# Key and small columns of a hybrid layer through one dense tile, with one latent step moved among the inverse's levels

## The reference, cut to what matters

```python
proj = rmsnorm(x, norm1_g) @ w_in
(ssd_z, ssd_xbc, ssd_dt, mla_cq, mla_ckv, mla_kr, gdn_qkv, gdn_z, gdn_b, gdn_a, gate_logits) = split(proj)
y_ssd = ssd_mixer(ssd_z, ssd_xbc, ssd_dt, ...)      # decays from dt, 16 heads
y_mla = mla_mixer(mla_cq, mla_ckv, mla_kr, ...)     # latents 512 + 256, rotary key 64
y_gdn = gdn_mixer(gdn_qkv, gdn_z, gdn_b, gdn_a, ...)# inverse of a lower triangle, per head and chunk
```

## Time and profile before

| | us |
|---|---|
| median of 3 runs | 2484.85 (2478.69 to 2486.74) |
| the profiled execution | 2484.22 |
| its span, first to last instruction | 2482.4 |
| PE busy | 2391.7 |
| mean granted clock of PE | 0.987 |

### The profile page before, as it was taken

How to read it: one execution, slowest core, us unless ns; L and a number is a source line. 1 busy time by engine, 2 the same in 40 slices (tenths; PEclk the granted TensorE clock), 3 DMA queues, 4 the chain that set the end, 5 groups by cost and what they waited for, 6 DMA issues and landing times.

```text
span 2482.4 us, 48243 instructions
## 1 busy us (share of the span) xinstructions
PE 2391.7 (96%) x21350; PEld 2217.1 (89%) x21350; DVE 1424.7 (57%) x2157; ACT 1249.5 (50%) x1848; POOL 302.0 (12%) x171
## 2 busy tenths in 40 slices
PE   7989999999999899999999999999999999998999
PEld 6979998999999799899999886887789997788999
DVE  5773776665457467756655347643335554676554
ACT  5755655554466475456543367532223444354442
POOL 4214000000241220001000004200000001331000
PEclk9999999999999999999999999999999999999999
DMA  4344444555444443545553245333225532223554
GB/s 175 136 154 170 153 160 171 197 187 187 157 169 152 154 157 139 199 154 194 190 186 128 102 138 203 124 120 131 103 101 188 203 139 103 87 76 131 187 187 170
DMA packets 56064, 382.31 MB, mean 154 GB/s; under 512 B 6064, under 2 KB 9904, under 8 KB 10288
## 3 DMA queue, kind: packets, MB, share of 16 engines
q1 hardware_dynamic: 55104, 375.90, 42.2%
q10 hardware_dynamic: 752, 3.33, 0.4%
HBM read 377.11 MB, written 1.05 MB: 152 GB/s over the span
## 4 chain that ended last, share of the span: by engine, by line
PE 82%; DVE 9%; ACT 4%; DMA 2%; issue 2%; POOL 0%; DVEq 0%; ACTq 0%; POOLq 0%
PE ps L948 21%; PE ps L949 21%; PE ps L950 21%; DVE r L2226 3%; ACT r L1567 2%; PE ps L1029 1%; PE ps L1077 1%; PE ps L1031 1%; PE ps L1030 1%; DMA ring<-in_win 1%; PE ps L907 1%; PE ps L869 1%; PE ps L986 1%; PE ps L988 1%; PE ps L987 1%
## 5 line engine op out<-in xcount | busy, mean ns | idle before, releaser
L948 PE MATMUL ps<-r,r 128*128 128x256 f32 (+1 forms) x4464 | 1326.2, 297 | 5.3 <-DVE r L2283 1.9
L949 PE MATMUL ps<-r,r 128*128 128x256 f32 (+1 forms) x4464 | 1313.1, 294 | 0.0
L950 PE MATMUL ps<-r,r 128*128 128x256 f32 (+1 forms) x4464 | 1311.7, 294 | 1.0 <-issue 1.0
L2226 DVE TENSOR_TENSOR r<-ring,r 128x1024 fp32r<-128x1024 f32 (+2 forms) x558 | 677.6, 1248 | 519.6 <-ACT r L1567 519.4
L948 PEld LDWEIGHTS ps<-r,r 128*128 128x128 f32 x4464 | 842.4, 189 | 42.1 <-issue 9.5
L950 PEld LDWEIGHTS ps<-r,r 128*128 128x128 f32 x4464 | 842.0, 189 | 25.0
L949 PEld LDWEIGHTS ps<-r,r 128*128 128x128 f32 x4464 | 842.4, 189 | 24.2 <-issue 0.5
L1567 ACT ACTIVATE r<-ring 128x1024 fp32r<-128x1024 f32 (+1 forms) x614 | 613.2, 1039 | 294.5 <-DMA ring<-in_fo 69.3
L3164 POOL TENSOR_TENSOR slab<-slab 128x512 f32<-128x512 f32 (+1 forms) x20 | 28.6, 1432 | 1231.2 <-ACT slab L1683 1210.9
L3116 POOL TENSOR_TENSOR r<-ring,r 128x1024 fp32r<-128x1024 f32 x56 | 133.2, 2400 | 226.3 <-ACT r L1567 216.4
L2315 DVE SCALAR_TENSOR_TENSOR slab<-ps,v,slab 128x255 f32<-128x255 f32 (+1 forms) x168 | 68.0, 474 | 81.6 <-ACT slab L1635 81.6
(11 more groups left out here) (344 smaller groups left out, 2530.1 us busy)
## 6 DMA issues: line engine op xcount, KB each, us to landing
ring<-in_win SPq DMA_DIRECT2D x76, 1024.0 KB, 4.8
ring<-in_ada SPq DMA_DIRECT2D x48, 1024.0 KB, 4.8
ring<-in_fi SPq DMA_DIRECT2D x44, 1024.0 KB, 4.8
ring<-in_fo SPq DMA_DIRECT2D x36, 1024.0 KB, 4.8
ring<-in_wup SPq DMA_DIRECT2D x32, 1024.0 KB, 4.7
ring<-in_wdn SPq DMA_DIRECT2D x32, 1024.0 KB, 4.8
ring<-in_hin SPq DMA_DIRECT2D x20, 1024.0 KB, 4.8
ring<-in_nqkv SPq DMA_DIRECT2D x12, 1024.0 KB, 4.8
```

The source lines that it names most:

```text
L948: self.mm(o, hi[:, k - k0, cs], xh, k == 0, False)
L949: self.mm(o, hi[:, k - k0, cs], xl, False, False)
L950: i = self.mm(o, lo[:, k - k0, cs], xh, False, k == last)
L2226: self.tt(K.low(p), K.raw(p), K.high(p).bitcast(F32), ALU.subtract).then_inc(*self.up("w_lo_v", p))
```

## The change

The 32 small columns and the 64 of the rotary key become one chunk of 128 columns (32 of them zero). It is computed as a dense tile, and ACT writes it to `few`, a free tile of `gate`. PE then turns the two token halves for `sm` (bank `smT`) and spreads the key's halves over the partitions by 8 matmuls with columns of the identity (bank `kr`), which ACT copies into `lat`'s tiles 6 and 7. `win` has 74 chunks instead of 76, and `lat` three steps instead of four. In the list of turns, the 5th piece of `small` comes one `qkv` step later and the rest of it after `qk`'s first piece, the first latent step goes from behind the recurrence to between the first and second level of the inverse, with its chunks prepared ahead of the first level, and the two others stay among the decays.

```diff
--- before.py
+++ after.py
@@ -28,7 +28,7 @@
 
 
 MATS = {
-    "win": (1024, 9728, 128, 1), "wsm": (1024, 32, 32, 1), "wuq": (512, 1536, 256, 1), "wuk": (256, 1024, 512, 1),
+    "win": (1024, 9472, 128, 1), "wsm": (1024, 128, 128, 1), "wuq": (512, 1536, 256, 1), "wuk": (256, 1024, 512, 1),
     "wuv": (256, 1024, 512, 1), "wso": (1024, 1024, 128, 1), "wmo": (1024, 1024, 128, 1), "wgo": (1024, 1024, 128, 1),
     "wo": (1024, 1024, 128, 1), "wup": (1024, 4096, 128, 1), "wdn": (4096, 1024, 128, 4),
     "ada": (1024, 6144, 128, 1), "nqkv": (1024, 3072, 128, 1), "no": (1024, 1024, 128, 1),
@@ -407,6 +407,7 @@
         self.xn = self.pair(A, 8, T)
         self.mixed, self.gate, self.y, self.sq, self.rs = (A(8, T) for _ in range(5))
         self.one = self.mixed[:, 0, 0:128]
+        self.few = self.gate[:, 1:2, :]
         self.sm, self.sp, self.sa, self.sb_, self.sc = A(2, 32), A(2, 24), A(2, 24), A(2, 24), A(2, 24)
         self.smask = A(48)
         self.beta, self.dA, self.cum = A(2, 8), A(2, 24), A(2, 24)
@@ -514,16 +515,16 @@
         win = lambda key, c0, c1, kind, **more: J.update({key: Job((key, L), "win", L, range(c0, c1), T, self.xn, n1, kind, **more)})
         out = lambda key, ys, kind, **more: J.update({key: Job((key, L), key, L, range(8), T, ys, halves((key, L)), kind, source=self.y, **more)})
         win("qkv", 0, 16, "conv", lead=2, dst=self.g_acc, taps="gw", bias=None, free=[])
-        J["wsm"] = Job(("wsm", L), "wsm", L, [0], 32, self.xn, n1, "rows", to=[self.sm[:, m, :] for m in range(2)])
-        win("z", 44, 52, "act", dst=self.g_z, func=ACT.Silu)
-        win("gz", 36, 44, "act", dst=self.z2, func=ACT.Silu, fine=True, free=lambda g: [("gd_v", ("y", L, 6))])
-        win("gate_g", 68, 76, "act", dst=self.mixed, func=ACT.Sigmoid)
+        J["wsm"] = Job(("wsm", L), "wsm", L, [0], T, self.xn, n1, "act", dst=self.few, func=ACT.Copy)
+        win("z", 42, 50, "act", dst=self.g_z, func=ACT.Silu)
+        win("gz", 34, 42, "act", dst=self.z2, func=ACT.Silu, fine=True, free=lambda g: [("gd_v", ("y", L, 6))])
+        win("gate_g", 66, 74, "act", dst=self.mixed, func=ACT.Sigmoid)
         out("wgo", self.ys_g, "mix", source_at=lambda i: ("gd_v", ("y", L, i)), gate=self.mixed, gate_of=("gate_g", L), first=True)
         win("xbc", 16, 28, "conv", dst=self.s_acc, taps="cw", bias="cb", free=[("gd_v", ("qg", L, 1, 1)), ("gd_p", ("uu", L, 3))])
-        win("lat", 28, 36, "act", dst=self.lat, func=ACT.Copy)
-        win("gate_s", 52, 60, "act", dst=self.gate, func=ACT.Sigmoid)
+        win("lat", 28, 34, "act", dst=self.lat, func=ACT.Copy)
+        win("gate_s", 50, 58, "act", dst=self.gate, func=ACT.Sigmoid)
         out("wso", self.ys_s, "mix", source_at=lambda i: ("sd_v", ("y2", L, i)), gate=self.gate, gate_of=("gate_s", L), first=False)
-        win("gate_m", 60, 68, "act", dst=self.gate, func=ACT.Sigmoid, free=lambda g: [("ev_v", ("gated", ("wso", L), g))])
+        win("gate_m", 58, 66, "act", dst=self.gate, func=ACT.Sigmoid, free=lambda g: [("ev_v", ("gated", ("wso", L), g))])
         J["wuq"] = Job(("wuq", L), "wuq", L, range(6), T, self.qn, xk(("qn", L)), "copy", dst=self.q12)
         J["wuk"] = Job(("wuk", L), "wuk", L, range(2), T, self.kn, xk(("kn", L)), "copy", dst=self.kT)
         J["wuv"] = Job(("wuv", L), "wuv", L, range(2), 512, self.kn, xk(("kn", L)), "rows", to=[self.vt[:, m, :] for m in range(2)])
@@ -572,20 +573,20 @@
         yield ("ada0", 1)
     first = lambda turn: [turn] if L == 0 else []
     yield from [("norm1", None), ("qkv", 2), ("small", 1), ("qkv", 1), ("small", 2), *first(("angles", 1)), ("qkv", 1), ("small", 1), *first(("angles", 1)),
-                ("qkv", 1), ("small", 1), *first(("angles", 1)),
-                ("qkv", 1), ("small", None), *first(("conditions", None)), ("qk", 1), ("qkv", 1), ahead("z", 1), ("qk", None), ("qkv", 1), ahead("z", 3),
+                ("qkv", 1), *first(("angles", 1)),
+                ("qkv", 1), ("small", 1), *first(("conditions", None)), ("qk", 1), ("qkv", 1), ahead("z", 1), ("small", None), ("qk", None), ("qkv", 1), ahead("z", 3),
                 ("qkv", None), ("z", 2), ahead("z", 5), ("gdn", 1), ahead("z", 7)]
     for fill in ("z", "z", "gate_g", "gate_g"):
         yield from [("gdn", 1), (fill, 1)]
     yield from [("gdn", 1), ("gate_g", 1), ("gdn", 1), ("gate_g", 1), ("gate_s", 1), ("gdn", 1), ("gate_s", 1),
-                ("gdn", 1), ("gate_s", 1), ("ada0", 2), ("gdn", 4), ahead("gate_s", 6), ("ada0", 1), ("gdn", 4), ahead("gate_s", 7),
+                ("gdn", 1), ("gate_s", 1), ("ada0", 2), ahead("lat", 1), ("gdn", 4), ("ada0", 1), ("lat", 1), ahead("gate_s", 6), ("gdn", 4), ahead("gate_s", 7),
                 ("gdn", 4), ("ada0", 1)]
     yield from [("gate_s", 1), ("gdn", 1), ("xbc", 1)]
     for n in range(5):
         yield from [("gdn", 1), ("xbc", 1)]
         if n in (0, 2):
             yield ("ada0", 1)
-    yield from [ahead("lat", 3), ("gdn", 1), ("xbc", 1), ("lat", 1), ("xbc", 1), ("lat", 1), ahead("lat", 5), ("gdn", None), ahead("lat", 7), ("ssd", 1)]
+    yield from [ahead("lat", 3), ("gdn", 1), ("xbc", 1), ("xbc", 1), ("gdn", None), ahead("lat", 5), ("ssd", 1)]
     for fill in ("lat", ("lat", "split wgo"), None, "wgo", "wgo", ("mla", "wgo"), None, "wgo"):
         yield ("ssd", 1)
         if fill:
@@ -1080,7 +1081,15 @@
 
     def small(self, L):
         K, up, at, e = self.K, self.up, self.at, self.e
-        yield from self.rows(K.jobs1[L]["wsm"])
+        yield from self.dense(K.jobs1[L]["wsm"])
+        P = self.open("smT", L)
+        self.wait_ge(*at("ev_s", ("wsm", L), 0))
+        self.turn(P, [K.few[:, 0, 128 * m:128 * m + 128] for m in range(2)]).then_inc(*up("sm_p", "T", L))
+        P = self.open("kr", L)
+        for r in range(2):
+            for q in range(0, 128, 32):
+                i = self.mm(P[q:q + 32, 256 * r:256 * r + 256], K.C["ident"][:, 32 * r:32 * r + 32], K.few[:, 0, :], True, True)
+        i.then_inc(*up("sm_p", "kr", L))
         yield
         yield
         yield
@@ -1807,15 +1816,20 @@
 
     def small(self, L):
         K, up, at, mine = self.K, self.up, self.at, self.mine
-        yield from self.rows(K.jobs1[L]["wsm"])
+        yield from self.dense(K.jobs1[L]["wsm"])
+        self.wait_ge(*at("sm_p", "T", L))
+        self.act(K.sm, self.bank("smT", L)[:, 0:256].rearrange("p (a b) -> p a b", a=2)[:, :, 64:96], ACT.Copy).then_inc(*up("sm_s", "sm", L))
+        self.emptied("sm_s", "smT", L)
+        self.wait_ge(*at("sm_p", "kr", L))
+        self.act(K.lat[:, 6:8, :], self.bank("kr", L).rearrange("p (a b) -> p a b", a=2), ACT.Copy).then_inc(*up("sm_s", "kr", L))
+        self.emptied("sm_s", "kr", L)
         yield
 
         self.e.preload_act_table_set(LN_EXP)
         self.wait_ge(*at("sm_v", "sp", L))
         self.act(K.sa, K.sp, ACT.Abs).then_inc(*up("sm_s"))
         self.act(K.ea, K.V1[L]["alog"], ACT.Exp).then_inc(*up("sm_s", "a", L))
-        for n, c in K.jobs1[L]["wsm"].copies:
-            self.wait_ge(*at("ev_s" if n == 0 else "ev_v", "row", ("wsm", L), n, c))
+        self.wait_ge(*at("sm_s", "sm", L))
         self.act(K.beta, K.sm[:, :, 24:32], ACT.Exp, scale=-1.0).then_inc(*up("sm_s", "beta", L))
         self.wait_ge(*mine("sm_s"))
         self.act(K.sa, K.sa, ACT.Exp, scale=-1.0).then_inc(*up("sm_s", "exp", L))
@@ -1976,7 +1990,7 @@
         K, up, at, mine = self.K, self.up, self.at, self.mine
 
         qn, kn, rs = ("qn", L), ("kn", L), K.rs
-        self.wait_ge(*at("ev_s", ("lat", L), 6))
+        self.wait_ge(*at("ev_s", ("lat", L), 4))
         self.power_own(qn, K.lat[:, 0:4, :], T)
         self.power_own(kn, K.lat[:, 4:6, :], T)
         yield
@@ -2761,7 +2774,8 @@
 
 
         self.wait_ge(*at("misc_s", "sin"))
-        self.wait_ge(*at("ev_s", ("lat", L), 6))
+        self.wait_ge(*at("sm_s", "kr", L))
+        self.wait_ge(*at("ev_s", ("lat", L), 4))
         rope(K.lat[:, 6:7, :], K.lat[:, 7:8, :], 1)
         yield
 
@@ -3339,9 +3353,8 @@
     win = a["w_in"]
     z, xbc, dt, cq, ckv, kr, qkv, gz, gb, ga, gate = np.split(
         win, np.cumsum([1024, 1536, 16, 512, 256, 64, 2048, 1024, 8, 8]).tolist(), axis=-1)
-    r1, r2 = np.tile(kr[..., 0:32], (1, 1, 4)), np.tile(kr[..., 32:64], (1, 1, 4))
-    d["win"] = tiled("win", np.concatenate([qkv, xbc, cq, ckv, r1, r2, z, gz, gate], -1))
-    d["wsm"] = tiled("wsm", np.concatenate([dt, ga, gb], -1))
+    d["win"] = tiled("win", np.concatenate([qkv, xbc, cq, ckv, z, gz, gate], -1))
+    d["wsm"] = tiled("wsm", np.pad(np.concatenate([kr, dt, ga, gb], -1), ((0, 0), (0, 0), (0, 32))))
     uq = a["mla_w_uq"].reshape(2, 512, 8, 192)
     d["wuq"] = tiled("wuq", np.concatenate([uq[..., 0:128].reshape(2, 512, 1024), uq[..., 128:160].reshape(2, 512, 256),
                                             uq[..., 160:192].reshape(2, 512, 256)], -1))
```

## The result

The changed kernel takes 2492.97 us (median of 8 runs, 2488.96 to 2498.72), the kernel before 2483.14 (8 runs, 2478.69 to 2486.74): ratio 1.0036, 95% interval 1.0024 to 1.0048. I had said 2480 and 2463 to 2490. The profiled execution took 2490.61 us, its span 2488.8 (before: 2484.22 and 2482.4).

A forecast was written before the change was run, and what follows sets the result against it. PE, busy 96% with 82% of the chain, was taken as the bound. Start -12.0 plus rest +6.8 (work -5.6, levels +2.8, decays +6.2, twice) gave -5.2 from 2484.22: 2479.0, said as 2480, range 2463 to 2490.

The forecast's parts named there:

- Start of the layers: Small columns, key, clock, running sums and a late chunk at each layer's start: -8.7 us in layer 0, -3.3 in layer 1.
- Tile, key products and clock: At the small columns: dense tile -2.6 us a layer, spreading the key +1.3, clock falls gone, -7.9 us for both layers.
- chunk 8 late: At the layer's start, PE waits for the low part of chunk 8 from POOL: +1.0 us in each layer.
- The dense subtraction for the small chunk: DVE's subtraction grows from 256 to 1024 columns at the layer's start; taken as hidden, bounds 0 and +1 us.
- Up to chunk 7 I find no wait: At the layer's start, PE's faster pace was held to meet no late low or high parts through chunk 7.
- The sums later: Running sums one `qkv` step later cover PE's wait for `dA` and its clock loss: -3.5 us, layer 0 alone.
- no wait in layer 1: PE was held not to wait for `dA` before layer 1's running sums, so moving them gains nothing there.
- The step among the levels: Latent step moved between the inverse's levels: +8.4 us a layer for 5.6 of work, 2.8 of waits net; bounds -5.6, +7.
- the stall without a releaser: In the first level, PE's 2.02 us wait for nothing the profile shows; half taken back, bounds 0 and 2.
- The decays: Stretch from output statistics to `wgo`: -5.0 us a layer for 11.3 of steps removed, 6.2 of waits added; bounds 0, 8.
- Rival 2: Idle PE keeps the clock at half through the first two levels and latent step: 8.2 us a layer, 2496; chance 0.12.
- rival 3: At the layers' start the clock falls whatever stands there: 2488, no change; chance 0.11.

The follow-up runs named there:

- e7: e1 with VectorE instead of GpSimd making the low parts of chunks 8 to 15 at the start of each layer; ratio to the kernel before 0.9949.
- e9: e7 with the sine of the angles two to three dense steps later, in layer 0 alone; 2468.93 us, ratio to the kernel before 0.9933.
- e1: The changed kernel with its latent steps back at their old places, dense tile and later sums kept; ratio to the kernel before 0.9966.
- e6: e1 with the running sums back one dense step earlier, at their old place; ratio to the kernel before 0.9994.
- e8: The changed kernel with 44 useless matmuls ahead of the second latent step behind the output statistics; ratio to the kernel before 1.0016.
- e3: The changed kernel with the moved latent step prepared behind the first level's four pieces, not ahead of them; ratio to the kernel before 1.0014.
- e2: The kernel before, narrow small columns kept, with only the first latent step moved among the levels; ratio to the kernel before 1.0074.

## Why the prediction was wrong, point by point

- **Start of the layers, said -12.0, came -4.1** (-3.6 and -0.5). This is the step that failed most. Tile, key products and clock were right: 1.07 us for the key, no half clock at the small columns, chunk 8 late by 0.95 and 0.80 for 1.0. The dense subtraction for the small chunk, taken as hidden, was: it took 3.23 us in layer 1 beside GpSimd, and PE did not wait for it. The failure is the sentence "Up to chunk 7 I find no wait" carried on to the end: I followed GpSimd only up to chunk 8. Behind it stand the waits of 2.24 us in layer 0 and 0.92 in layer 1 (which has two more of 0.44 and 0.59) and 2.8 us of half clock in layer 0, of which the same code shows between 0 and 2.8; so some 1 us of this profile's miss is its own bad luck. I had the blocked operation before me in the earlier trace rows and weighed it for one subtraction only, not for the dA chain. That it was the block, e7 and e9 show: with the low parts on VectorE the operations take 0.2 us, and layer 1's start is 3.8 and 3.7 us shorter than in e1.
- **The sums later, said -3.5 in layer 0 and nothing in layer 1.** By e6 against e1 the edit is worth 6.4 us in layer 1's start, where it covers a lateness that the tile brought, and 1.5 in layer 0's, which is within what the same code shows. The step that failed is "no wait in layer 1": it was read from the kernel before, not from the one with the tile.
- **The step among the levels, said +8.4 a layer, came +10.8 and +8.5.** Right in mechanism and, in layer 1, in size. In layer 0 the transfer took 7.1 us and not the 6.2 of the earlier trace rows, and with the half clock five of the eight groups of turned copies took 1.1 us for 0.66, where two did before. That the size came nearer in layer 1 is partly luck: the same code gave 33.7 to 36.7 us there. Of the stall without a releaser I gave back half; all of it went.
- **The decays, said -5.0, came -3.7 and -3.6.** Wait and place were right (5.56 us for the 5.6 worked out). The stretch was forecast at 20.7 us and took 22.0: the step behind the wait took 1.7 and 1.8 us longer at half clock, a term that the sum put at nothing without a reason. e8 shows that this half clock is the idle time's, and has the 20.7.
- **Rival 2** had the right sign and the right place for the half clock, but not its length: it ended at 173.7, and the latent step at 174.3 was at full clock. Of its 8.2 us a layer the 4.6 for that step did not come. The median lies between rival 3 (2488) and rival 2 (2496), and neither is what happened.
- **The sum.** Start +7.9, levels +2.5, decays +2.7 against the forecast, and -1.5 in the rest: 11.6, which is 2490.6 for 2479.0. One slip in the working did no harm: the third level is called 3.6 us, the rows give 3.4, and the 8.3 added for both levels is right.

Not settled: 1 to 2 us of the start of layer 1, and whether the clock's falls in the rest answer to the edits or vary by themselves. Also open is what holds PE in the stall that no releaser explains: it is gone in the changed kernel and back in e3, with 1.90 and 3.05 us.

## What to carry to other kernels

Ask of a stretch what its longest chain is before taking work out of it or moving work in: behind the statistics ScalarE and VectorE set the end as soon as one step was gone, so the first step taken out gave 4.6 us at best (e1) and the second nothing. That chain holds the preparation of the steps itself, and where it stands counts: with it ahead of the scaling the first step gave 1.4 us (e2). When a change makes PE faster, follow every engine that feeds it until the pace is steady again; the pauses that closed were what let small VectorE operations through at 0.2 us and not 2.35. Price the clock with the wait: behind 5.56 us of idle PE the next step took 1.7 us more. And before a difference of 1 or 2 us in a stage is explained, look at the same stage in kernels that run the same code there.

## What was not expected of the hardware

VectorE's small operations were held by GpSimd's subtraction, one of them with a single SBUF input (TENSOR_SCALAR, 2.41 us for 48 elements), and only one operation of VectorE got through between two of GpSimd, so that four of them took 9.4 us. Six taps, which read PSUM, took 2.43 us beside the same GpSimd row. Behind one and the same wait of 2.1 to 2.3 us, in five kernels with the same code, the clock cost 0, 1.6 (three times) or 2.8 us; behind waits of 5.55 to 6.08 us it cost 1.6 to 2.5 us all six times.
